# Two trunk panels prepared during attention, and the attention's projection pieces in three places of a step instead of two

## The reference

```python
def diff_attention(h, w_qkv, w_o, ...):
    q, k, v = jnp.split(h @ w_qkv, 3, axis=-1)
    q = rope(q.reshape(B, S, 8, 2, 64), positions) * 64 ** -0.5
    k = rope(k.reshape(B, S, 8, 2, 64), positions)
    ...
        s = jnp.einsum('bqhcd,bkhcd->bhcqk', qb, k)       # two maps per head
        s = jnp.where(allowed[None, None, None], s, -jnp.inf)   # causal in chunks of 64
        p = jax.nn.softmax(s, axis=-1)
        a = p[:, :, 0] - lam * p[:, :, 1]
        return jnp.einsum('bhqk,bkhe->bqhe', a, v)
    ...
    o = rmsnorm(o, subln_g, SUBLN_EPS) * (1.0 - lambda_init)
    return o.reshape(B, S, 1024) @ w_o

x = x + diff_attention(rmsnorm(x, mix_norm_g[0]), ...)
x = x + sqrelu_mlp(rmsnorm(x, mlp_norm_g[0]), mlp_w1[0], mlp_w2[0])
```

## Time and profile before

| | us |
|---|---|
| median of 3 runs | 3884.37 |
| the runs | 3870.95 to 3885.73 |
| the profiled execution | 3856.3 |
| its span, first to last instruction | 3854.4 |
| of it: steps 1 to 47 of attention, with projection | about 110 to 500 |
| of it: steps 48 to 63 and the last outputs | about 500 to 599 |
| first matmul of the trunk | 610.53 |

### The profile page before, as it was taken

The page is one execution under the profiler, slowest core; times in us unless marked ns, Lnnn a source line. Parts: engine busy times, 40 slices in busy tenths (PEclk is TensorE's granted clock), DMA queues, the critical chain, the costliest instruction groups (busy, mean ns, idle before and its releaser), DMA issues. The chain is left out here.

```text
span 3854.4 us, 43829 instructions
## 1 busy us (share of the span) xinstructions
PE 3585.1 (93%) x17560; PEld 2804.3 (73%) x17560; DVE 1647.4 (43%) x1906; ACT 1089.5 (28%) x1652; POOL 1148.0 (30%) x666
## 2 busy tenths in 40 slices
PE   7999987999999999999999999799969979997897
PEld 6777756888888888788888888687625758763565
DVE  4666754312121259642111113566536531463653
ACT  2444452101010116521010111115426310442540
POOL 2454502333332336523332333222202122230211
PEclk9999988999999999999999999899989989998998
DMA  4243312111111121211111111141042121202311
GB/s 157 93 138 131 118 58 92 45 49 49 46 47 49 60 82 47 85 49 49 47 46 49 49 49 38 50 136 55 12 136 56 61 98 44 77 23 82 99 61 60
DMA packets 80124, 267.18 MB, mean 69 GB/s; under 512 B 9424, under 2 KB 10608, under 8 KB 79984
## 3 DMA queue, kind: packets, MB, share of 16 engines
q1 hardware_dynamic: 54464, 191.30, 15.2%
q10 hardware_dynamic: 18608, 48.78, 3.7%
q0 software_dynamic: 6912, 25.17, 2.0%
HBM read 214.62 MB, written 46.40 MB: 68 GB/s over the span
## 5 line engine op out<-in xcount | busy, mean ns | idle before, releaser
L674 POOL CAST tk_w_hi<-tk_w_raw 128x1024 fp32r<-128x1024 f32 x160 | 178.0, 1112 | 1196.6 <-PE tk_acc L191 550.1
L191 PE MATMUL tk_acc<-tk_b_hi,tk_w_hi 128*128 128x512 f32 x1280 | 397.4, 392 | 11.4 <-POOL tk_w_lo L676 11.4
L191 PE MATMUL tk_acc<-tk_a_hi,tk_w_hi 128*128 128x512 f32 x1280 | 398.1, 392 | 3.2 <-POOL tk_w_lo L676 2.5
L191 PE MATMUL tk_acc<-tk_b_hi,tk_w_lo 128*128 128x512 f32 x1280 | 399.6, 394 | 0.0
L191 PE MATMUL tk_acc<-tk_a_hi,tk_w_lo 128*128 128x512 f32 x1280 | 399.5, 394 | 0.0
L676 POOL TENSOR_TENSOR tk_w_lo<-tk_w_raw,tk_w_hi 128x1024 fp32r<-128x1024 f32 x160 | 394.2, 2464 | 12.8
L191 PE MATMUL tk_acc<-tk_b_lo,tk_w_hi 128*128 128x512 f32 x1280 | 397.6, 392 | 0.0
L191 PE MATMUL tk_acc<-tk_a_lo,tk_w_hi 128*128 128x512 f32 x1280 | 397.4, 392 | 0.0
L828 ACT ACTIVATE tk_sq<-tk_r 128x1024 f32<-128x1024 f32 x64 | 67.8, 1060 | 1078.9 <-DVE tk_r L957 1078.9
L932 DVE TENSOR_TENSOR xT<-tk_acc,xT 128x1024 f32<-128x1024 f32 x80 | 98.0, 1225 | 605.5 <-PE tk_acc L191 605.5
L191 PEld LDWEIGHTS tk_acc<-tk_b_hi,tk_w_hi 128*128 128x128 f32 x1280 | 241.0, 188 | 66.0 <-POOL tk_w_lo L676 11.8
(11 more groups left out here) (392 smaller groups left out, 6753.8 us busy)
## 6 DMA issues: line engine op xcount, KB each, us to landing
tk_w_raw<-in_w_trunk SPq DMA_DIRECT2D x160, 512.0 KB, 3.3
da_w_mod<-in_ada_w POOLq DMA_DIRECT2D x48, 512.0 KB, 3.7
pj_w_raw<-in_w_in SPq DMA_DIRECT2D x44, 512.0 KB, 3.3
da_w_raw<-in_w_qkv SPq DMA_DIRECT2D x24, 512.0 KB, 3.6
x_dram<-xT ACTq DMA_DIRECT2D x24, 512.0 KB, 4.6
ma_w_raw<-in_w_out SPq DMA_DIRECT2D x16, 512.0 KB, 3.9
xT<-x_dram SPq DMA_DIRECT2D x16, 512.0 KB, 8.0
qk_dram<-xT ACTq DMA_DIRECT2D x26, 256.0 KB
```

The source lines that it names most:

```text
L191: last = pe.matmul(self.acc[:, u, s * HALF:(s + 1) * HALF], w[:, u, k, :], h[:, k, s * HALF:(s + 1) * HALF], start=(k == order[0] and part ...
L674: pool.tensor_copy(pn.hi[:, u, :, :], pn.raw[:, u, :, :]).then_inc(sems[f"w_hi{u}"], 1)
```

## The change

Two parts. First, the two-slot panel buffers `w_raw`, `w_hi`, `w_lo` are allocated once around attention and trunk (`held`). SP loads the trunk's panels 0 and 1 into them behind its last q and k loads of attention, as soon as all 12 splits of a slot are done; GpSimd splits them at step 48, after V's last block. The trunk's loops for loading and splitting begin at 1, with the semaphores of turn 0 raised by hand. Second, `middle(j)` becomes `third(j, n)`: a step's units are issued in three parts, the first now between `scores(t + 1)` and `transposes(t, 0)`; `window(t)` goes from first third to first third; and ScalarE does the `take_v` that are due before `copies(t, 0)` instead of after the first exponential.

```diff
@@ -123,19 +123,22 @@
-    def __init__(self, nc, sems, sb, ps, w, n_panels, kc, prep=None, naturals=0, room=None, acc=None):
+    def __init__(self, nc, sems, sb, ps, w, n_panels, kc, prep=None, naturals=0, room=None, acc=None, held=None):
         self.naturals = naturals
         self.nc, self.sems, self.w, self.pairs, self.kc, self.prep = nc, sems, w, n_panels // 2, kc, prep
-        self.raw = sb("w_raw", [P, 2, kc, P])
-        self.hi = sb("w_hi", [P, 2, kc, P], F32R)
-        self.lo = sb("w_lo", [P, 2, kc, P], F32R)
+        if held is not None:
+            self.raw, self.hi, self.lo = held
+        else:
+            self.raw = sb("w_raw", [P, 2, kc, P])
+            self.hi = sb("w_hi", [P, 2, kc, P], F32R)
+            self.lo = sb("w_lo", [P, 2, kc, P], F32R)
         self.acc = acc if acc is not None else ps("acc", [P, 2, S])
         self.splits = [(self.hi, self.lo)] * 2
         if naturals:
             self.splits[1] = tuple(room[:, j:j + 2, :].rearrange("p u (k n) -> p u k n", k=kc) for j in (0, 2))
-    def load(self, sync):
-        with sync.Fori(0, self.pairs) as i:
+    def load(self, sync, begin=0):
+        with sync.Fori(begin, self.pairs) as i:
             for u in range(2):
                 sync.wait_ge(self.sems[f"w_split{u}"], i + 1)
@@ -617,7 +620,7 @@
                             self.add_square(dve, sems, sq[:, :], 2 * i + u)
-    def trunk(self, oT):
+    def trunk(self, oT, held):
@@ -645,7 +648,7 @@
             rstd = sb("rstd", [P, S])
             sp = sb("sp", [P, 5, DK])
             aux = ps("aux", [P, 2, S])
-            pn = Panels(nc, sems, sb, ps, self.ins["w_trunk"], 160, DK)
+            pn = Panels(nc, sems, sb, ps, self.ins["w_trunk"], 160, DK, held=held)
             rr, pad, gt = r[:, 0:S], r[:, 0:S + 3], self.acc[:, :]
             A, B = (a_hi, a_lo), (b_hi, b_lo)
@@ -660,12 +663,16 @@
             by_pool = [n < 3 for n in range(DK)]
             with nc.Block() as block:
-                block.sync(pn.load)
+                @block.sync
+                def _(sync):
+                    pn.load(sync, 1)
                 @block.gpsimd
                 def _(pool):
                     for u in range(2):
-                        pool.sem_inc(sems[f"w_split{u}"], 1)
+                        pool.sem_inc(sems[f"w_landed{u}"], 16)
+                        pool.sem_inc(sems[f"w_hi{u}"], 1)
+                        pool.sem_inc(sems[f"w_split{u}"], 2)
                     def weights(turn, u):
                         pool.wait_ge(sems[f"w_landed{u}"], 16 * turn + 16)
@@ -700,7 +707,7 @@
                             pool.tensor_tensor(b_lo[:, n, :], gt, b_hi[:, n, :].bitcast(F32), ALU.subtract)\
                                 .then_inc(sems["y_lo_pool"], 1)
-                    with pool.Fori(0, R_X // 2) as i:
+                    with pool.Fori(1, R_X // 2) as i:
                         for u in range(2):
                             weights(i, u)
                     order = {1: [(block_weights, 0), (block_weights, 1)], 3: [(branch_low, 0), (branch_low, 1)],
@@ -2054,7 +2061,7 @@
-    def attention_layer(self):
+    def attention_layer(self, held):
@@ -2081,15 +2088,15 @@
             return sum(1 if b < 4 else 2 for _, b in blocks[:t])
-        def middle(j):
-            return CUT[j] + (CUT[j + 1] - CUT[j]) // 2
+        def third(j, n):
+            return CUT[j] + (CUT[j + 1] - CUT[j]) * n // 3
         def window(t):
             j = t % STEPS
             if j == 0:
-                return t // STEPS, middle(STEPS - 1), ALL
-            return t // STEPS + 1, middle(j - 1), middle(j)
+                return t // STEPS, third(STEPS - 1, 1), ALL
+            return t // STEPS + 1, third(j - 1, 1), third(j, 1)
         def pieces(t):
@@ -2104,9 +2111,7 @@
         with nc.sbuf_tensor("at_under", [P, DK, S], F32), nc.sbuf_tensor("oT", [P, DK, S], F32) as oT:
             pass
         with self.parts("a"), stage(nc, "da", names) as (sems, sb, ps):
-            w_raw = sb("w_raw", [P, 2, DK, P])
-            w_hi = sb("w_hi", [P, 2, DK, P], F32R)
-            w_lo = sb("w_lo", [P, 2, DK, P], F32R)
+            w_raw, w_hi, w_lo = held
             pr = sb("pr", [P, 2, 2, S])
             pts = sb("pts", [P, S])
             v = sb("v", [P, 2, SB, 256])
@@ -2209,6 +2214,10 @@
                         if hp + 1 < pairs:
                             weights(hp + 1, 0)
                         load(2 * hp + 1)
+                    for u in range(2):
+                        sync.wait_ge(sems[f"w_split{u}"], 3 * pairs)
+                        sync.dma_start(w_raw[:, u, :, :].rearrange("p k n -> p (k n)"), self.ins["w_trunk"][u])\
+                            .then_inc(sems[f"w_landed{u}"], 16)
                     sync.wait_ge(sems["fv"], SB * pairs)
                     for u in range(units - 2):
                         for f in range(2):
@@ -2263,6 +2272,9 @@
                         mod_load(n)
                     for t in range(nb):
                         hp, j = t // STEPS + 1, t % STEPS
+                        if hp == pairs and j == 0:
+                            for u in range(2):
+                                split(pairs, 0, u)
                         if hp < pairs:
                             if j == 0:
                                 split(hp, 0, 0)
@@ -2419,12 +2431,14 @@
                         filled = 0 < hp < pairs
                         if t >= 0:
                             scores(t + 1)
+                        if filled:
+                            fill(hp, CUT[j], third(j, 1))
                         transposes(t, 0)
                         if filled:
-                            fill(hp, CUT[j], middle(j))
+                            fill(hp, third(j, 1), third(j, 2))
                         transposes(t, 1)
                         if filled:
-                            fill(hp, middle(j), CUT[j + 1])
+                            fill(hp, third(j, 2), CUT[j + 1])
                         values(t)
                         for u, f in out_due(t):
                             if t < nb:
@@ -2614,11 +2628,14 @@
                     act.activation(lam_d[:, 2:4], lam_d[:, 0:2], ACT.Exp).then_inc(sems["lam"], 1)
                     act.wait_ge(sems["silu"], 1)
                     for t in range(-1, nb + 7):
+                        hp, due = v_blocks(t)
+                        for n in due:
+                            take_v(hp, n)
                         copies(t, 0)
                         exps(t + 1, 0)
-                        hp, due = v_blocks(t) if t >= 0 else (0, range(EARLY, SB))
-                        for n in due:
-                            take_v(hp, n)
+                        if t < 0:
+                            for n in range(EARLY, SB):
+                                take_v(0, n)
                         copies(t, 1)
                         exps(t + 1, 1)
                         scale_weights(t)
@@ -2668,7 +2685,9 @@
 def build(nc, ins, out):
     with ExitStack() as ctx:
         m = Model(nc, ctx, ins, out)
-        m.trunk(m.attention_layer())
+        with nc.sbuf_tensor("held_raw", [P, 2, DK, P], F32) as raw, nc.sbuf_tensor("held_hi", [P, 2, DK, P], F32R) as hi, \
+                nc.sbuf_tensor("held_lo", [P, 2, DK, P], F32R) as lo:
+            m.trunk(m.attention_layer((raw, hi, lo)), (raw, hi, lo))
         m.mixed_layer(0)
         m.mixed_layer(1)
         m.final_norm("n5", "fin_g2", "out")
```

## The result

The changed kernel took 3831.95 us (median of 4 runs, 3824.49 to 3836.56), the kernel before beside it 3879.7 us (4 runs, 3870.95 to 3885.73). The ratio is 0.9898, 95% interval 0.9867 to 0.9928: faster by 1.0%. The prediction was 3877.2 us, range 3861 to 3891, with 0.85 on a change within half a per cent. Both were wrong. Executions of one kernel scatter here by up to 43 us, so medians and single profiles are read apart.

A forecast was written before the change was run, and what follows sets the result against it. TensorE, busy 93%, was taken as the bound, so only its idle stretches or extra work counted. Gains of 15.6 us less costs of 8.4, net 7.2, took 3884.4 to 3877.2 us, range 3861 to 3891.

The forecast's parts named there:

- the part on bounds: Whole kernel: TensorE busy 93%, so only its idle stretches or extra work count; the change touches attention and the seam.
- The part on the two panels: Trunk panels loaded and split during attention: loads delay nothing, GpSimd's split at steps 48 and 49 costs 0.5 us.
- the signs of being wrong: Scores waiting on exponentials, combine waits at steps 49 or 50, unchanged seam release, or 110-500 us longer or over 10 shorter.
- The transposes' waits: Attention: transposes' waits for combined probabilities shrink, gain 6.3 us; waits at steps 16 and 32 grow to 1.4, cost 2.1.
- V's bank waits: Attention, V projection: all seven waits for a bank ScalarE has not emptied go, gain 5.2 us, at least 3.
- The last V block's place: Steps 16, 32 and 48: emptying V's block 7 leaves ScalarE's line before the second copy, gain 1.1 us.
- The extra piece: Attention: one more run of projection matmuls in 45 steps, 0.1 us each, cost 4.5 us (3.6 to 9).
- all waits go and the extra run is free: Rival, chance 0.15: in attention the extra-run cost and possibly the step 16/32 cost vanish; net 13.8 us, 3870.6.
- The split at unit 192: Attention, step 11: TensorE waits 0.4 us for the second V panel's low part, three times, cost 1.3 us.
- The scores behind the exponentials: Rival "slower", chance 0.10: attention scores wait for the second exponential; at 0.3 us a step 6.3 us slower, 3890.7.
- The lock at steps 48 and 49: GpSimd's split blocks VectorE's combines: cost 0.5 us; as rival, chance 0.10, two blocked by 2.0 each, 3880.7.
- The seam: Between attention and trunk: TensorE starts sooner, released by VectorE's low part, gain 3.0 us (1.5 to 4).

The follow-up runs named there:

- thirds: The kernel before with only the projection pieces in three places and V's blocks taken first, panels at their old offset; 3860.1 us, 0.9967 of before.
- place: The kernel before with only the panel buffers held in front of both stages, loads, splits and order untouched; 3842.8 us, 0.9943 of before.
- shift320: The kernel before with an unused 320-byte tensor in front of the trunk's panel buffers; 3844.7 us, 0.9930 of before.
- preload: The kernel after with its pieces back in two places, held buffers and two early panels kept; 3844.2 us, 0.9937 of before.
- pad64: The kernel before with 64 unused bytes ahead of the trunk's panels; 3846.1 us, 0.9935 of before.
- thirds_again: The kernel before with only the three places and V taken first, unchanged from its first run and executed once more; 3844.6 us, 0.9948 of before.
- take_first: The kernel before with ScalarE taking V's finished blocks ahead of its copies, pieces still in two places; 3867.8 us, 0.9998 of before.
- after_again: The kernel after, unchanged, executed once more; 3833.6 us, 0.9882 of before.
- place_thirds: The kernel before with held panel buffers and pieces in three places, without the two early panels; 3835.1 us, 0.9894 of before.
- before_again: The kernel before, unchanged, executed once more for another profile; 3857.0 us, 0.9984 of before.

## Why the prediction was wrong

**The step that failed** is the part on bounds. It begins with "So time can come only from stretches in which TensorE stands still, or from its extra work" and ends with "Everything else shifts with these two." The first takes TensorE's time for the same matmuls as fixed, and under the second lies a price of 0 for moving the panel buffers. In the profiled pair TensorE's busy time fell by 15.5 us with the same matmuls. The part on the two panels weighed when they come free, and not where they lie. The runs put -15.8 us of the trunk in its place (before at 228.9 ns against after), and -29.5 where the first MLP ran at the slower level (1829.3 us in `thirds` against 1799.8). In medians, `place`, `shift320`, `preload` and `pad64` are 0.57 to 0.70% faster than before, of 3870 us some 22 to 27 us. That is over half of the measured 1.0%. None of the four rivals had it. The bounds of the range were built from terms of attention and seam only, and so no width of theirs could reach it. Nor could the signs of being wrong that the prediction lists: the stretch with projection came out 8.7 us shorter in the profiled pair, inside the limit of 10, and the one sign that did come, a wait at step 49, is 1.0 us.

A row of before hinted at it. The first kind of trunk matmul had lowest, median and highest 387/392/794 ns, while at the good offset lowest and median are both 389. Also, the execution of the profile lay 28 us under the median of three runs. The prediction set this aside ("I use the difference alone"). By `thirds` and `thirds_again` 14 to 16 us of such a spread can stand in the trunk, and asking where it stands in the kernel would have led there.

**The transposes' waits** (predicted -6.3, and two waits of 1.4 at steps 16 and 32). The mechanism was right, and the two waits read 1.28 us each. Timeline row of T0(16), after:

```profile
232.85 0.66 PE L2363 MATMUL da_pt<-ident,da_pr 128*128 128x128 f32 x4 [1.28 <-DVE da_pr L2491]
```

Two errors of size nearly cancel. The profile of before showed 7.3 us of these waits, its second profile 11.5 and `place` 11.7: the term was read from an execution that happened to have few. Of 11.5 us, 6.5 are left. And three waits of 1.3 us at steps 10, 26 and 42 were not foreseen. There VectorE meets GpSimd twice in one step, timeline of after:

```profile
178.69 2.37 POOL L2246 TENSOR_TENSOR held_lo<-held_raw,held_hi 128x1024 fp32r<-128x1024 f32 x1
...
179.02 2.32 DVE L2490 TENSOR_SCALAR da_pr<-da_pr,da_st,da_neg_lam 128x512 f32<-128x512 f32 x1
...
181.03 2.55 POOL L2263 TENSOR_TENSOR da_mod_acc<-da_mod_acc,da_w_mod 128x1024 f32<-128x1024 f32 x1
...
181.38 2.75 DVE L2491 SCALAR_TENSOR_TENSOR da_pr<-da_pr,da_st 128x512 f32<-128x512 f32 x1
...
184.18 0.66 PE L2363 MATMUL da_pt<-ident,da_pr 128*128 128x128 f32 x4 [1.33 <-DVE da_pr L2491]
```

Each of the two VectorE operations ends only behind the GpSimd operation beside it, at 181.34 behind 181.06 and at 184.13 behind 183.58. The same two over 512 columns took 0.55 and 0.75 us at 502.05 and 502.63, once GpSimd had finished. The Trainium skill (SBUF — State Buffer, "SBUF: two separate sides") has such a lock held for a whole instruction; for the second operation, with two SBUF inputs, its condition and the row agree.

**V's bank waits** (-5.2): all seven gone, as said, and the term was too small. The view counts a wait only from the end of the matmul before. In V's products the matmuls last 0.28 us by their rows and start every 0.12 us, so the first part of a wait is hidden, and a short one altogether. Rows of before in step 47:

```profile
495.63 0.28 PE L2314 MATMUL da_x<-da_w_lo,a_h_hi 128*128 128x256 f32 x1
496.04 0.39 PE L2314 MATMUL da_x<-da_w_hi,a_h_hi 128*128 128x256 f32 x1
```

The starts are 0.41 us apart and no wait is printed. From the last mask matmul to P, less the counted waits, steps 12 to 15 took 5.59, 5.80, 6.03 and 6.38 us before and 5.40, 5.59, 5.81 and 6.02 after, and the steps of the next two pairs the same within 0.03. That is 3.0 us over the twelve steps, on top of the 5.2, although each has one more run of matmuls. `take_first` shows that the waits go for good only because the pieces moved as well.

**The last V block's place** (-1.1): right. Where P waited 1.1 us at each of steps 16, 32 and 48 it waits 0.7 now.

**The extra piece** (+4.5, 3.6 to 9). This term is wrong in size. Over T0(0) to T0(48), the windows of before and of after read:

```profile
107.00:502.70 395.70, 377.38 (x2304) 0.97 0.37 122
```

```profile
104.90:491.88 386.98, 374.43 (x2304) 0.97 0.38 128
```

The same 2304 matmuls keep TensorE busy no longer (374.43 us against 377.38), with 45 more runs. The clock doesn't hide the cost. At a granted clock of 0.974 five profiles with two places are busy 374.3 to 374.7 us and two with three places 373.3 and 373.4; at 0.965 the profile of before is busy 377.4 and three with three places 375.4 to 375.8. So at like clock three places are busy 0.9 to 2.0 us less. The steps say why. In sixteen pairs of like steps of before and after that have q or k units, no counted wait and the full clock, the time from mask to P grew by 0.03 to 0.09 us in fourteen and fell by 0.09 in two, 0.05 in the mean. Over the 33 such steps that is some 1.7 us (an estimate), and V's steps gave back 3.0, so the sum is about -1.3. An extra run costs about 0.07 us in most steps, near the 0.1 of the prediction; what the prediction missed is V's hidden waits, which more than pay for it.

Idle time is 21.2 us in the mean of five profiles with two places and 12.3 in that of eight with three: 8.9 less. The terms for waits inside this stretch were -6.3, -5.2, -0.7 (two of the three places of 0.37), +2.1 and +1.3, so -8.8: in the mean they were right. For the whole attention, T0(0) to last O, eight profiles of each kind differ by 9.4 us in the mean (493.0 and 483.6) where the terms gave 4.2 and the rival "all waits go and the extra run is free" (0.15) gave 13.8 - 3.0 = 10.8. That rival was nearer in size, but by another way: some waits stayed, and the extra run is not free.

**The split at unit 192** (+1.3): right, three waits of together 1.5 us, where one of 0.3 stood before. The view names no releaser, but each first matmul starts 0.1 us behind the end of GpSimd's low part (190.98 and 191.08, for one). **The scores behind the exponentials** (rival, 0.10): two waits of 0.5 us together; it fell. **The lock at steps 48 and 49** (+0.5; rival +4.0): one wait of 1.01 us at T0(49), behind a combine of 768 columns that took 1.67 and the one operation before it, 1.50:

```profile
498.92 0.66 PE L2363 MATMUL da_pt<-ident,da_pr 128*128 128x128 f32 x4 [1.01 <-DVE da_pr L2491]
```

It began within one of GpSimd's casts (496.67 to 498.05 us) and ended 0.81 us behind it: it was held up for the rest of one short operation, and the combine of the step before was not late. The term was half a microsecond too small, the rival too large. From T0(48) to last O after took 97.2 us and before 96.0.

**The seam** (-3.0): measured -2.6 in the stretch and 2.64 in the idle time (11.37 to 8.73), released as foreseen by VectorE's low part. `preload` against `place` has 2.9, `after_again` against `place_thirds` 3.0. Without the early panels, though, the seam takes 11.8 us in five profiles and 12.8 to 12.9 in six (`before_again` among them), and with them 8.7 to 9.2 in six. The gain is thus 3.5 us in the mean, inside the 2.2 to 4 of the prediction, and no median alone could show it.

**The balance.** Of the prediction's own terms the profiled pair shows -7.6 and -2.6, 10.2 us in place of 7.2. The trunk adds 15.8 in this pair and 14 more where the first MLP of the execution before has the slower level. Start (-2.1) and rest (+5.6) differ between executions of kernels that are alike there by as much: with the mixed layers as they were, the rest took 1426.1 to 1430.1 us in ten profiles and 1431.1 to 1437.8 in five, and `place`, which moves the same buffers, is among the ten; T0(0) came at 104.1 to 107.2. 4 to 5 us of it stand in the first mixed layer's attention, and there the granted clock differs, of before and then of after:

```profile
2877.60:3127.30 249.70, 233.32 (x1440) 0.99 0.20 61
```

```profile
2852.00:3107.00 255.00, 238.82 (x1444) 0.97 0.19 57
```

Of the fifteen profiles eight took 249.6 to 250.1 us there at 0.99, six 254.4 to 254.9 at 0.97, and one lies between. The offset doesn't sort them (`place` is in the first group, `preload` in the second). Why the clock falls in some executions and not in others is open.

## What to carry to other kernels

Moving a buffer is an edit of its own: before pricing a change at its place in the program, compare where each tensor lies before and after, and test the new place alone, as an unused tensor of a few hundred bytes does in one line. If a long, regular stretch of matmuls has a median duration above the lowest, or if runs of one kernel scatter by one per cent, look at the interval of that stretch first, and in parts of the stretch, since a mean can hide two levels; it was worth 25 us in the trunk and 12 in the mixed layers. Look at the products of other widths too: what was best for 512 columns was not best for 256. A wait removed on one engine comes back at the next join unless that join gets cover as well, and waits of a microsecond should be summed over more than one execution before they are priced, by the distance of starts where matmuls overlap. Before two executions are compared within a few microseconds, compare their granted clocks.
